# Two transformer blocks in one kernel: the first piece's high part on the vector engine, a ninth warm-up, the fourth unit's split ahead of the first squares, and the last reciprocal ahead of a wait

## The reference

```python
def rmsnorm(x, w):
    xf = x.astype(jnp.float32)
    y = xf * lax.rsqrt(jnp.mean(xf * xf, axis=-1, keepdims=True) + EPS)
    return (y * w.astype(jnp.float32)).astype(x.dtype)
...
    for l in range(DEPTH):
        h = rmsnorm(x, attn_norm_w[l])
        proj = h @ w_in[l]
        (q_a, k_a, v_a, q_b, k_b, v_b, g_b, g_c, x_c) = jnp.split(proj, split_points, axis=-1)
        y_sb = from_heads(stick_breaking_attention(to_heads(q_a), to_heads(k_a), to_heads(v_a)))
        qh = rmsnorm(to_heads(q_b), q_norm_w[l])
        kh = rmsnorm(to_heads(k_b), k_norm_w[l])
        y_ch = from_heads(chunked_relpos_attention(qh, kh, to_heads(v_b), rel_bias[l]))
        y_cv = short_conv_mixer(g_b, g_c, x_c, conv_w[l])
        y = group_rmsnorm(jnp.concatenate([y_sb, y_ch, y_cv], axis=-1), out_norm_w[l])
        x = x + y @ w_out[l]
        x = x + swiglu(rmsnorm(x, ffn_norm_w[l]), w_gate[l], w_up[l], w_down[l])
```

## Time and profile before

| | us |
|---|---|
| median of 3 timed runs | 695.68 |
| lowest, highest | 694.89, 696.22 |
| the profiled execution, whole | 695.99 |
| its span, first to last instruction | 694.0 |
| PE busy | 685.1 (99%) |
| PE weight loads busy | 602.7 (87%) |
| DVE busy | 498.4 (72%) |
| ACT busy | 401.6 (58%) |
| DMA, mean rate | 179 GB/s |

### The profile page before, as it was taken

One profiled execution on the slowest core, in us unless ns is written; L12 is line 12 of the kernel. 1 busy time (PEld: TensorE's weight loads), 2 busy tenths in 40 slices (PEclk: granted clock), 3 DMA queues, 4 the chain that ended last, 5 costly groups with the idle time before them and its releaser, 6 DMA issues.

```text
span 694.0 us, 10061 instructions
## 1 busy us (share of the span) xinstructions
PE 685.1 (99%) x4118; PEld 602.7 (87%) x4118; DVE 498.4 (72%) x689; ACT 401.6 (58%) x504; POOL 9.4 (1%) x25
## 2 busy tenths in 40 slices
PE   8999999999999999999999999999999999999996
PEld 7889999888888888888878888899978888888885
DVE  5866677979986766666565477687779988886353
ACT  6875866755555554464457565564557666664342
POOL 1000000003000000000000000000000000000000
PEclk9999999999999999999999999999999999999999
DMA  8863225655565555545435346454555655554511
GB/s 322 316 232 135 90 93 183 220 183 193 179 219 187 194 182 182 187 178 193 171 124 180 122 138 226 160 181 146 182 211 182 203 184 189 200 196 175 190 60 61
DMA packets 19773, 124.05 MB, mean 179 GB/s; under 512 B 2320, under 2 KB 3472, under 8 KB 5520
## 3 DMA queue, kind: packets, MB, share of 16 engines
q1 hardware_dynamic: 18432, 120.07, 48.8%
q10 hardware_dynamic: 1296, 3.35, 1.4%
HBM read 122.36 MB, written 1.05 MB: 178 GB/s over the span
## 4 chain that ended last, share of the span: by engine, by line
PE 90%; DVE 4%; ACT 3%; issue 1%; DMA 1%; DVEq 0%; ACTq 0%
PE psum L1601 34%; PE psum L1602 18%; PE psum L1594 10%; PE psum L1596 10%; PE psum L1595 10%; PE psum L1590 2%; DVE wlo L978 2%; ACT whi L525 2%; PE psum L1641 1%; PE psum L2073 1%; PE psum L1647 1%; PE psum L1644 1%; DMA x<-in_xT 1%; PE psum L2121 0%; DVE gates L1496 0%
## 5 line engine op out<-in xcount | busy, mean ns | idle before, releaser
L978 DVE TENSOR_TENSOR wlo<-raw,whi 128x2048 fp32r<-128x2048 f32 x110 | 251.7, 2290 | 78.2 <-ACT whi L525 78.1
L525 ACT CAST whi<-raw 128x2048 fp32r<-128x2048 f32 x110 | 209.7, 1908 | 44.7 <-PE psum L1596 38.4
L1601 PE MATMUL psum<-hx,whi 128*128 128x512 f32 x528 | 183.6, 391 | 0.0
L1602 PE MATMUL psum<-hx,wlo 128*128 128x256 f32 x528 | 148.9, 282 | 0.0
L1601 PE MATMUL psum<-yx,whi 128*128 128x512 f32 x352 | 123.3, 393 | 1.1 <-DVE yx L989 1.0
L1601 PEld LDWEIGHTS psum<-hx,whi 128*128 128x128 f32 x528 | 99.1, 188 | 20.9 <-issue 0.2
L1602 PEld LDWEIGHTS psum<-hx,wlo 128*128 128x128 f32 x528 | 99.8, 189 | 0.0
L1602 PE MATMUL psum<-yx,wlo 128*128 128x256 f32 x352 | 99.2, 282 | 0.0
L1601 PEld LDWEIGHTS psum<-yx,whi 128*128 128x128 f32 x352 | 66.0, 188 | 15.7 <-DVE yx L989 2.1
L1602 PEld LDWEIGHTS psum<-yx,wlo 128*128 128x128 f32 x352 | 66.5, 189 | 0.0
L1601 PE MATMUL psum<-G,whi 128*128 128x512 f32 x176 | 61.8, 393 | 0.0
(11 more groups left out here) (271 smaller groups left out, 1107.0 us busy)
## 6 DMA issues: line engine op xcount, KB each, us to landing
raw<-in_stream SPq DMA_DIRECT2D x110, 1024.0 KB, 4.7
raw<-in_stream SPq DMA_DIRECT2D x8, 256.0 KB, 5.5
relb<-in_relb ACTq DMA_DIRECT2D x1, 1536.0 KB, 9.7
raw<-in_stream SPq DMA_DIRECT2D x2, 512.0 KB, 7.7
x<-in_xT SPq DMA_DIRECT2D x3, 256.0 KB, 5.5
out_t<-sq SPq DMA_DIRECT2D x4, 160.0 KB, 2.4
final_gain<-in_final_gain ACTq DMA_DIRECT2D x1, 512.0 KB, 3.5
bsp<-in_bsp ACTq DMA_DIRECT2D x1, 384.0 KB, 3.4
```

The source lines that it names most:

```text
L525: act.copy(whi[s][:], raw[s][:]).then_inc(unit_hi, 1)
L978: dve.tensor_tensor(wlo[s][:], raw[s][:], whi[s][:], ALU.subtract).then_inc(unit_lo, 1)
L1601: pe.matmul(bank[b][:], stat[0], mov, start=first, stop=False, skip_group_check=True)
L1602: return pe.matmul(bank[b][:, 0:T], stat[1], mov[:, 0, :], start=False, stop=last, skip_group_check=True)
```

## The change

Six places change:

- The high part of the first piece is made by DVE (`tensor_copy`, with a semaphore `first_hi` of its own), and DVE makes its low part before the low part of x's first chunk. ACT's loop leaves that piece out, and the counts on `piece_hi` are one lower.
- `WARM_UP` is 9 instead of 8.
- `split(3)`, the fourth unit, stands behind the last piece on ACT and DVE, ahead of ACT's squares and DVE's folding, instead of behind them.
- On ACT, `split(4)` stands behind the bias table's DMA issue and `root(0)`, instead of ahead of both.
- On PE, `stats(0)` stands behind unit 2 instead of in its middle.
- In `final_scale`, the product by the gain is issued without a wait for it; the reciprocal follows at once and waits for ACT's root alone, and the wait for the product stands ahead of the two scales.

```diff
-WARM_UP = 8
+WARM_UP = 9
...
@@ scalar block @@
             for k in range(KT):
                 act.wait_ge(x_loaded[next(c for c, (a, b) in enumerate(X_CHUNKS) if a <= k < b)], 16)
                 h_high("attn_norm", k)
-                split_piece(k)
+                if k:
+                    split_piece(k)
             split_piece(8)
             split_piece(9)
+            split(3)
             for b in range(4):
                 square2(b)
...
             for n in range(1, len(IN1)):
-                if n == 1:
-                    split(3)
                 if n == 2:
-                    split(4)
                     act.dma_start(relb[:], A["relb"]).then_inc(bias_loaded, 16)
                     root(0)
+                    split(4)
                     act.wait_ge(r_ready, 1)
...
@@ vector block @@
             dve.wait_ge(consts, 1)
-            for k in range(KT):
+
+            dve.wait_ge(piece_loaded[0], 16)
+            dve.tensor_copy(whi[0][:, 0:WIDE], raw[0][:, 0:WIDE]).then_inc(first_hi, 1)
+            split_piece(0)
+            h_low("attn_norm", 0, 0)
+            for k in range(1, KT):
                 h_low("attn_norm", 0, k)
                 split_piece(k)
             split_piece(8)
             split_piece(9)
+            split(3)
             fold(0)
...
             for n in range(1, len(IN1)):
-                if n == 1:
-                    split(3)
...
             def final_scale(t):
+                final_gained(2 + t).then_inc(dve_order, 1)
+                n_order[0] += 1
                 dve.wait_ge(final_root, t + 1)
                 dve.reciprocal(root_out[:, t:t + 1], root_out[:, t:t + 1]).then_inc(final_r, 1)
+                dve.wait_ge(dve_order, n_order[0])
                 dve.wait_ge(final_r, t + 1)
...
             final_add(2)
-            done(final_gained(2))
             final_scale(0)
...
-            done(final_gained(3))
             final_scale(1)
...
@@ tensor block, first_unit @@
-                    pe.wait_ge(*((unit_hi, u + 1) if last else (piece_hi, pieces_before(u) + 1 + kk)))
+                    if k == 0:
+                        pe.wait_ge(first_hi, 1)
+                    else:
+                        pe.wait_ge(*((unit_hi, u + 1) if last else (piece_hi, pieces_before(u) + kk)))
...
@@ tensor block, halfway and the loop over the units @@
-                if n == 2:
-                    stats(0)
...
+                if n == 2:
+                    stats(0)
```

More of the change, by code:

```diff
@@ L324, in build @@
         piece_loaded = [sem(f"piece_loaded{q}") for q in range(len(PIECES))]
-        piece_hi, piece_lo = sem("piece_hi"), sem("piece_lo")
+        first_hi, piece_hi, piece_lo = sem("first_hi"), sem("piece_hi"), sem("piece_lo")
         unit_loaded = [sem(f"unit_loaded{s}") for s in range(RING)]
@@ L982, in split_piece @@
                 s = u % RING
-                dve.wait_ge(*((unit_hi, u + 1) if b == UNIT else (piece_hi, pieces_before(u) + 1 + a // (b - a))))
+                if q == 0:
+                    dve.wait_ge(first_hi, 1)
+                elif b == UNIT:
+                    dve.wait_ge(unit_hi, u + 1)
+                else:
+                    dve.wait_ge(piece_hi, pieces_before(u) + a // (b - a))
                 dve.tensor_tensor(wlo[s][:, a:b], raw[s][:, a:b], whi[s][:, a:b], ALU.subtract)\
```

## The result

| us | before | changed |
|---|---|---|
| median (8 runs each) | 695.72 | 697.44 |
| lowest, highest | 694.81, 696.22 | 696.93, 698.67 |
| profiled execution, span | 694.0 | 695.8 |
| PE busy in it | 685.1 | 685.1 |

The ratio is 1.003, 95% interval 1.0019 to 1.0041: the change made the kernel slower by 1.7 us, against a forecast of 1.64. The spans of the two profiled executions differ by 1.78 us, and two places account for 1.71 of it: PE's first transposes come 2.07 us later, and the tail behind the start of the last matmul is 0.36 us shorter. The other 0.07 us lie between the two.

The account below looks back on a forecast made before the run. The prediction took PE (TensorE) to bound the kernel. Transposes 1.99 us later, less 0.35 at the last reciprocal, gave +1.64 on 695.68, so 697.3 us (chance 0.50), range 695.3 to 698.4.

Parts of the forecast that it names:

- PE bounds the middle, so a shift in the first 40 us is passed on: Start of the kernel: any delay or gain of PE in the first 40 us reaches the end whole.
- 0.52 us of slack before the transposes: Before turn_b: DVE's product ends at 32.77 us, transposes start at 33.29, the tightest place in PE's early stretch.
- First matmul at 5.07, copy 0.48 us: Kernel start: DVE copies the first piece in 0.48 us, PE's first matmul comes at about 5.07, 0.47 us earlier.
- Unit 3's landing holds ACT, the squares and the statistics: ACT waits for unit 3 at 18.1 us; squares end at 22.15, folding at 24.42, PE waits until 24.45.
- Unit 4 behind the root adds the second wait: Before the transposes: DVE's low part of unit 4 starts at 27.79, 2.46 us later, so turn_b starts at 35.28.
- The gain of the start is swallowed: The two start edits' 1.2 us is lost in PE's wait before the statistics; turn_b starts 17.14 us after unit 3's landing.
- The reciprocal, -0.35: Kernel's end: without the wait for the product, the 0.40 us between root and last reciprocal shrinks, saving 0.35 us.
- Sum +1.64: Whole kernel: turn_b 1.99 us later, less 0.35 at the last reciprocal, makes it 1.64 us slower.
- Rival B: Start: before's timed runs got the upper clock later than the profiled one; 0.8 us won back, 696.5 us; chance 0.20.
- C: Start: unit 3 lands earlier, at 15.0 us turn_b comes at 32.1 and the time is 694.1 us; chance 0.09.
- D: The clock falls in PE's two new waits and costs 1.7 us more, 699.0 us; chance 0.06.
- E: A later wait takes up most of the 2 us, or reciprocal wins and start loses less: 695.5 to 696.3; chance 0.15.

Follow-up runs that it names:

- Unit 4 first: Changed kernel with ACT's `split(4)` back ahead of the bias load and `root(0)`: median 696.17 us, 1.12 below the changed kernel beside it.
- the order alone: Kernel before with only the moves of `split(3)`, `split(4)` and `stats(0)`, without start edits or reciprocal edit: median 697.85 us, 2.09 above before.
- again: The changed kernel run once more without an edit: median 697.29 us, 1.53 above the kernel before beside it.
- squares first: Changed kernel with `split(3)` back behind ACT's squares and DVE's folding: median 695.93 us, 0.02 below before, ratio 1.0013.

## Why the prediction was right, step by step

- **PE bounds the middle, so a shift in the first 40 us is passed on.** Right. From the turn to the last matmul's start it took 687.90 - 33.29 = 654.61 us before and 690.04 - 35.36 = 654.68 after.
- **0.52 us of slack before the transposes, "the tightest place in this stretch".** Wrong, and without effect on the sum. Unit 3's low part ended at 22.28 + 2.29 = 24.57 us, and PE took it up at 24.89, 0.32 us later:

```profile
24.89 0.40 PE L1594 MATMUL psum<-whi,hx 128*128 128x512 f32 x1
```

So in the order of before, with the loads as in that trace, the 1.2 us of the two start edits were out of reach; the three kernels with edits of the start alone ran into this place.
- **First matmul at 5.07, copy 0.48 us.** 4.97 and 0.43. The value that I scaled from a 384-column row was 0.05 too long, and decided nothing. The estimate by the Trainium skill, "VectorE: DVE Perf Modes", section "The perf-mode tier table", was 0.3 to 0.4, and the 0.43 us of the trace lie just above it.
- **Unit 3's landing holds ACT, the squares and the statistics.** Right to 0.05 us: cast at 18.13, low part at 20.07, folded 24.41 (24.42 forecast), statistics 24.46.
- **Unit 4 behind the root adds the second wait.** Right: low part of unit 4 at 27.85 (27.79), turn at 35.36 (35.28). The 0.08 us are the statistics' matmuls, which take a little longer behind a wait. "Unit 4 first" confirms its size alone, 1.07 us.
- **The gain of the start is swallowed.** Right, by "the order alone": the same distance of 17.23 us from unit 3's cast with and without the start edits.
- **The reciprocal, -0.35.** Right in size (-0.36 in the two tails), only half right in its reason. I took the gap to be that of the pair of waits, with the doubt that the wait had long been met. The edit does close the gap in the kernel before (0.45 to 0.03). But the same pair costs 0.10 us once the first piece is on DVE, so the pair alone is not the cause, and without the edit the first piece on DVE would have taken most of the gap away.
- **Sum +1.64.** Measured +1.72 and, again, +1.53. That the first lies within 0.1 us is in part luck. The sum takes the landing at 18.1 us, and the traced execution had just that; it is the longest of its eight, and by the spans these cost 1.1 to 1.3 us more than before. Some 0.4 us more outside the span brought the median to +1.72.
- **Rival B** was partly true: before's spans lie from 693.0 to 694.7 and the clock rose at 9.1 to 10.4 us in four traces of kernels whose start is that of before, but at 4.9 in "the order alone", whose start is the same too. So the moment does differ from run to run, as the Trainium skill, "TensorE: Matmul & The Clock Gate", section "Part 1: The HAM clock gate", has it. Its mechanism is in the traces of the order of before: the clock came up at 9.1, 9.3, 9.4 and 10.4 us and the turn stood at 33.29, 33.35, 33.40 and 33.89. It did not bring the change to "no difference", since the profiled run of before was near the middle of its spans (694.0; the medians beside the experiments are 694.0, 694.0 and 694.2). **C** fell: the landing was never before 17.3 us. **D** fell for the changed kernel: neither trace shows a fall behind its waits, and its 19 runs had a granted clock of 0.998 to 0.999. For the three long runs of "squares first" it stays open. **E** found no support.

## What to carry to other kernels

Before moving a step ahead of others in an in-order list, look at when its own input arrives: here a cast moved ahead of work that could fill the time until its load had landed, and everything behind it was then timed by the load's arrival. An edit that brings the bounding engine forward is worth only as much as the next just-in-time input allows; follow each of these in turn (unit 3's low part, the folded squares, the heads' product) and move them together. Where a small gap is put down to a wait that had long been met, check whether it survives in a program whose instructions are merely shifted.

## What the runs showed of the hardware

- A gap of 0.36 to 0.47 us ahead of one DVE instruction stood in all five traces of four programs. It was 0.10 us in two programs that differ in a copy, a wait and the order of two instructions 680 us earlier in DVE's list.
- The same kernel start (gap of 0.6 to 0.7 us between warm-up and first matmul of the projection) got the full clock at 9.1, 9.3, 9.4 and 10.4 us in four traces and at 4.9 us in a fifth. With the first matmul at 4.8 to 5.1 us it came between 4.1 and 6.8 us in eight traces.
- The clock fell to 0.50 in a wait of PE of 3.90 us and was full again at 29.5 us, 5.8 us behind the wait's end; it did not fall in any of the waits of 0.87 to 1.45 us.
- The same 1 MB load, issued at 9.5 to 10.7 us, landed between 17.3 and 18.1 us over fourteen traces of twelve programs; in two traces each of before and of the changed kernel, at 18.14 and 18.07, and at 18.10 and 17.46.
